# The GLA stage of a hybrid decoder step in another order: early output tiles between the near products

## What is computed

```
def rec_mixer(...):
    hm, c, n, m = mlstm_chunkwise(...)
    hm = rms_norm(hm, m_norm_g) * jax.nn.sigmoid(mo)
    log_a = jax.nn.log_sigmoid((glr @ w_gate_up + b_gate)) / G_GATE_TAU
    hg, s = gla_chunked(gq * G_KEY_DIM ** -0.5, gk, gv, log_a, s0)
    hg = rms_norm(hg, g_norm_g) * jax.nn.silu(gg)
    mix = jnp.concatenate([hm, hg], axis=-1)
    return mix @ w_out, c, n, m, s

def gla_chunked(q, k, v, log_a, s0):       # one chunk of it
    bc = jnp.cumsum(lac, axis=2)
    o_inter = einsum('bhtk,bhkv->bhtv', qc * exp(bc), s)
    decay = exp(where(mask, bc[:, :, :, None, :] - bc[:, :, None, :, :], -inf))
    a = einsum('bhtk,bhsk,bhtsk->bhts', qc, kc, decay)
    o = o_inter + einsum('bhts,bhsv->bhtv', a, vc)
    s_new = exp(b_end)[..., None] * s + einsum('bhsk,bhsv->bhkv', kc * exp(b_end - bc), vc)
```

## Time and profile before

| | us |
|---|---|
| median of 3 runs | 1524.04 |
| lowest, highest | 1517.58, 1527.65 |
| the profiled execution | 1523.02 |
| its span in the trace | 1521.4 |
| mean granted clock of TensorE | 0.957 of full |
| PE busy (matmul) | 1421.0 (93%) |
| DVE busy | 844.3 (55%) |
| ACT busy | 524.2 (34%) |
| POOL busy | 100.4 (7%) |

### The profile page before, as it was taken

How to read it: one execution, slowest core, us unless ns; L and a number is a source line. 1 busy time by engine, 2 the same in 40 slices (tenths; PEclk the granted TensorE clock), 3 DMA queues, 4 the chain that set the end, 5 groups by cost and what they waited for, 6 DMA issues and landing times.

```text
span 1521.4 us, 29729 instructions
## 1 busy us (share of the span) xinstructions
PE 1421.0 (93%) x11874; PEld 1349.3 (89%) x11874; DVE 844.3 (55%) x1277; ACT 524.2 (34%) x856; POOL 100.4 (7%) x138
## 2 busy tenths in 40 slices
PE   5999999788999999999999898997799999999997
PEld 4889899678999999999998677775699999999997
DVE  5355357564666666623253777778446666665221
ACT  4333434334333232322233454554243332322110
POOL 0021111112000000000000000000020000000000
PEclk9899999779999999999999999997799999999999
DMA  5443243212222223322126666773022222233320
GB/s 199 70 144 80 99 113 107 53 59 84 79 88 97 86 93 94 120 96 91 59 91 209 183 221 193 220 252 129 22 95 93 88 97 85 94 99 109 113 90 21
DMA packets 45820, 167.86 MB, mean 110 GB/s; under 512 B 5882, under 2 KB 7210, under 8 KB 45498
## 3 DMA queue, kind: packets, MB, share of 16 engines
q1 hardware_dynamic: 38506, 143.77, 29.0%
q0 software_dynamic: 7248, 23.15, 6.1%
HBM read 155.42 MB, written 11.48 MB: 110 GB/s over the span
## 4 chain that ended last, share of the span: by engine, by line
PE 84%; DVE 6%; issue 4%; ACT 4%; DMA 1%; POOL 0%; DVEq 0%; ACTq 0%; POOLq 0%
PE ps L516 55%; PE ps L567 13%; PE ps L696 2%; DVE mx L2084 1%; PE ps L925 1%; PE ps L1028 1%; ACT w_hi L1097 1%; ACT e_att L1455 1%; PE ps L631 1%; PE ps L879 1%; PE ps L1004 1%; PE ps L941 1%; PE ps L738 1%; PE ps L928 1%; DMA qb<-q_rows 1%
## 5 line engine op out<-in xcount | busy, mean ns | idle before, releaser
L516 PE MATMUL ps<-h_hi,w_hi 128*128 128x260 f32 x1616 | 459.4, 284 | 5.1 <-DVE h_lo L1562 4.6
L1553 DVE TENSOR_TENSOR w_lo<-raw,w_hi 128x1024 fp32r<-128x1024 f32 (+1 forms) x189 | 245.0, 1296 | 390.8 <-ACT w_hi L1097 390.8
L516 PE MATMUL ps<-h_hi,w_lo 128*128 128x260 f32 x1616 | 457.9, 283 | 0.0
L516 PE MATMUL ps<-h_lo,w_hi 128*128 128x260 f32 x1616 | 456.3, 282 | 0.0
L516 PEld LDWEIGHTS ps<-h_hi,w_hi 128*128 128x128 f32 x1616 | 305.4, 189 | 6.9 <-issue 4.4
L516 PEld LDWEIGHTS ps<-h_lo,w_hi 128*128 128x128 f32 x1616 | 305.2, 189 | 0.2
L516 PEld LDWEIGHTS ps<-h_hi,w_lo 128*128 128x128 f32 x1616 | 305.2, 189 | 0.0
L1097 ACT CAST w_hi<-raw 128x1024 fp32r<-128x1024 f32 (+1 forms) x189 | 208.0, 1101 | 224.3 <-PE ps L516 216.7
L516 PE MATMUL ps<-a_lo,w_hi 128*128 128x260 f32 x704 | 199.0, 283 | 0.0
L516 PE MATMUL ps<-a_hi,w_hi 128*128 128x260 f32 x704 | 198.8, 282 | 0.0
L516 PE MATMUL ps<-a_hi,w_lo 128*128 128x260 f32 x704 | 198.8, 282 | 0.0
(11 more groups left out here) (381 smaller groups left out, 2121.6 us busy)
## 6 DMA issues: line engine op xcount, KB each, us to landing
raw<-in_w_ffn SPq DMA_DIRECT2D x88, 512.0 KB, 3.4
raw<-in_w_down SPq DMA_DIRECT2D x32, 704.0 KB, 4.1
k_pages<-in_cache_k SPq DMA_DIRECT2D x32, 512.0 KB, 4.3
v_pages<-in_cache_v SPq DMA_DIRECT2D x32, 512.0 KB, 6.1
raw<-in_w_rec_in SPq DMA_DIRECT2D x29, 512.0 KB, 4.9
raw<-in_w_att_kv SPq DMA_DIRECT2D x24, 512.0 KB, 4.1
raw<-in_w_rec_out SPq DMA_DIRECT2D x8, 512.0 KB, 3.7
raw<-in_w_att_q SPq DMA_DIRECT2D x8, 512.0 KB, 3.5
```

Source lines behind the costliest of these rows:

```text
L516: ins = TE.matmul(half(bank, h), w_part[:, buf, w], m_part[:, k_at + k, h * HALF:(h + 1) * HALF], start=start, stop=stop)
L1553: V.tensor_tensor(w_lo[:, n % 2, 0:nk * P], raw[:, n % RAW, 0:nk * P], w_hi[:, n % 2, 0:nk * P].bitcast(F32), ALU.subtract).then_inc(lo_sp ...
```

## The change

It reorders and does not change what is computed.

- `early` becomes a generator that gives out one matmul at a time. `near_levels` takes such a generator and places one of its matmuls before every fourth near product. In pair 0 near A takes the last third (`h_lo` with `w_hi`) of early tiles 0 and 1, near B takes tile 2; in pair 1 near A takes tile 5, near B tile 6. What the generator has left after its 96 near products follows behind.
- Tiles 3, 4 and 7 are still done whole (`whole`), tile 3 behind `chunk_states(0)`, tile 4 behind `chunk_outputs(0)`, tile 7 ahead of `out_sums(1)`.
- `sample_outputs` moves from behind `chunk_outputs` to directly behind `within`.
- `exponents(0, "near")` moves ahead of the norm of the last mLSTM head on DVE, and `near_decays(0)` ahead of the conversion of the mLSTM rows on ACT.
- `sample_states` is split: its product (`sample_products`) moves ahead of `near`.
- In the late tiles the first halves of tiles 0 and 1 stand before the waits for the last GLA rows; the late tiles' PSUM banks are in another order (`LATE_BANK`).
- Splits of the slabs, and the drains, move to fit.

The core of the diff:

```diff
-            def early(m, bank, step=1):
+            def early(m, bank, step=1, terms=(0, 1, 2)):
...
+                            if t == 2 and k == KT // 2 - 1 and g == 1:
+                                ins.then_inc(slab_done if m % 2 else early_done, 1)
+                            yield
...
-            def near_levels(p, levels, at_bank):
+            def near_levels(p, levels, at_bank, beside, every):
...
                             for blk in range(4):
+                                if (4 * hh + blk) % every == every - 1:
+                                    next(beside, None)
...
-            early(0, 0)
+            whole(0, 0, terms=(0, 1))
...
-            early(1, 2, 5)
+            whole(1, 2, 5, (0, 1))
...
-                near_levels(p, (2, 3, 4), 3)
-                near_levels(p, (5, 6, 7), 5)
+                first, second = ((after_early(), early_behind(2, 2, 5, rD, "m1", 0)),
+                                 (early_behind(5, 0, 1, vA, "vt", 1), early_behind(6, 2, 5, oD, "tp1", 0)))[p]
+                near_levels(p, (2, 3, 4), 3, first, 4)
...
+                near_levels(p, (5, 6, 7), 5, second, 4)
...
-                if p:
-                    wait(pe, oD, "tp0", p - 1)
-                else:
-                    wait(pe, rD, "m1")
+                wait(pe, rD, "m6" if p else "m2")
...
             within(0)
+            sample_outputs(0)
+            chunk_states(0)
             wait(pe, gD, "n4", 0)
-            early(2, 3)
-            chunk_states(0)
-            wait(pe, rD, "m2")
-            early(3, 3)
-            chunk_outputs(0)
+            whole(3, 3)
             wait(pe, gA, "far", 0)
             v_chunks(1)
-            sample_outputs(0)
-            wait(pe, vA, "vt", 1)
-            early(4, 0)
+            chunk_outputs(0)
+            wait(pe, rD, "m3")
+            whole(4, 3)
             out_sums(0)
-            wait(pe, rD, "m4")
-            early(5, 0)
 
             within(1)
-            wait(pe, gD, "n4", 1)
-            early(6, 3)
+            sample_outputs(1)
             chunk_states(1)
             chunk_outputs(1)
-            sample_outputs(1)
+            wait(pe, gA, "far", 1)
+            whole(7, 0)
             out_sums(1)
-            wait(pe, gA, "far", 1)
-            early(7, 0)
             wait(pe, rD, "m7")
             wait(pe, oD, "lo1", 0)
             late(0, range(2))
-            wait(pe, oD, "lo0", 1)
-            late(0, range(2, 3))
-            wait(pe, oD, "lo1", 1)
-            late(0, range(3, 4))
             wait(pe, oA, "rms1", 1)
-            for c in range(1, S_OUT):
+            late(1, range(2))
+            for k in range(2):
+                wait(pe, oD, f"lo{k}", 1)
+                for c in range(2):
+                    late(c, range(2 + k, 3 + k))
+            for c in range(2, S_OUT):
                 late(c, range(KT // 2))
...
             size_of_decay(1)
             own_decay(0)
+            near_decays(0)
+            values(0)
             act.wait_ge(early_free, 1)
             wait(act, mD, "mix", M_HEADS - 1)
             S.copy(h_hi[:, 0:4, :], z[:, 12:16, :]).then_inc(hA.sem, 1)
-            values(0)
-            near_decays(0)
...
                     running(0)
+                    exponents(0, "near", 2, len(LEVELS))
                 rec_split(4)
```

More of the change, by code:

```diff
@@ L698, in early, with whole @@
                                             stop=t == 2 and k == KT // 2 - 1)
-                ins.then_inc(slab_done if m % 2 else early_done, 1)
+                            if t == 2 and k == KT // 2 - 1 and g == 1:
+                                ins.then_inc(slab_done if m % 2 else early_done, 1)
+                            yield
+            def whole(m, bank, step=1, terms=(0, 1, 2)):
+                for _ in early(m, bank, step, terms):
+                    pass
             def late(c, ks):
@@ L711, in late @@
                         for w_part, m_part in ((w_hi, h_hi), (w_hi, h_lo), (w_lo, h_hi)):
-                            ins = TE.matmul(half(2 * (c % 4), g), w_part[:, n % 2, w],
+                            ins = TE.matmul(half(LATE_BANK[c], g), w_part[:, n % 2, w],
                                             m_part[:, 4 + k, g * HALF:(g + 1) * HALF],
@@ L746, in _, with after_early, early_behind @@
             wait(pe, lA, "abs1")
-            early(1, 2, 5)
+            whole(1, 2, 5, (0, 1))
+            def after_early():
+                yield from early(0, 0, terms=(2,))
+                yield from early(1, 2, 5, (2,))
+            def early_behind(m, bank, step, steps, name, r):
+                wait(pe, steps, name, r)
+                yield from early(m, bank, step)
             def within(p):
@@ L756, in within @@
                     wait(pe, mA, "rms", M_HEADS - 1)
-                near_levels(p, (2, 3, 4), 3)
-                near_levels(p, (5, 6, 7), 5)
+                first, second = ((after_early(), early_behind(2, 2, 5, rD, "m1", 0)),
+                                 (early_behind(5, 0, 1, vA, "vt", 1), early_behind(6, 2, 5, oD, "tp1", 0)))[p]
+                near_levels(p, (2, 3, 4), 3, first, 4)
+                for _ in first:
+                    pass
+                near_levels(p, (5, 6, 7), 5, second, 4)
+                for _ in second:
+                    pass
                 wait(pe, dD, "qk_far", p)
@@ L786, in chunk_states @@
                 wait(pe, vA, "vt", p)
-                if p:
-                    wait(pe, oD, "tp1", p - 1)
                 for c in range(NC_G):
@@ L824, in out_sums @@
                 wait(pe, oA, "sq0", p)
-                wait(pe, rD, "m6" if p else "m3")
+                if p == 0:
+                    wait(pe, rD, "m4")
                 sums_of(3, 0)
@@ L1723, in cols_, with halves_of, exponents @@
                 return ap.unsqueeze(1).to_broadcast([P, n, ap.shape[1]])
+            def halves_of(ap, m):
+                v = ap.rearrange("p (n a m) -> p n a m", a=2, m=m)
+                return v[:, :, 0, :], v[:, :, 1, :]
+            def exponents(p, name, lo, hi):
+                wait(dve, dD, "bc", p)
+                if p:
+                    wait(dve, gP, "nearB" if name == "near" else "far", p - 1)
+                for l in range(lo, hi):
+                    m = LEVELS[l]
+                    early, late = halves_of(bc[:, :], m)
+                    to_early, to_late = halves_of(lev[:, l, :], m)
+                    edge = early[:, :, m - 1:m].to_broadcast([P, T // (2 * m), m])
+                    V.tensor_tensor(to_late, late, edge, ALU.subtract)
+                    ins = V.tensor_tensor(to_early, edge, early, ALU.subtract)
+                ins.then_inc(dD.sem, 1)
             def decay_input(p):
@@ L1831, in _ @@
                     rec_split(5)
-            def halves_of(ap, m):
-                v = ap.rearrange("p (n a m) -> p n a m", a=2, m=m)
-                return v[:, :, 0, :], v[:, :, 1, :]
-            def exponents(p, name, lo, hi):
-                wait(dve, dD, "bc", p)
-                if p:
-                    wait(dve, gP, "nearB" if name == "near" else "far", p - 1)
-                for l in range(lo, hi):
-                    m = LEVELS[l]
-                    early, late = halves_of(bc[:, :], m)
-                    to_early, to_late = halves_of(lev[:, l, :], m)
-                    edge = early[:, :, m - 1:m].to_broadcast([P, T // (2 * m), m])
-                    V.tensor_tensor(to_late, late, edge, ALU.subtract)
-                    ins = V.tensor_tensor(to_early, edge, early, ALU.subtract)
-                ins.then_inc(dD.sem, 1)
             def key_exponents(p):
@@ L1991, in _ @@
             end_factors(1)
-            early_drain(5, 0)
-            split("rec_out", 0, 3, KT)
+            sample_products(1)
             near(1)
-            early_drain(6, 3)
-            states(1)
+            early_drain(6, 2, 5)
             sample_states(1)
             split("rec_out", 0, 4, KT)
+            states(1)
             early_drain(7, 0)
@@ L2011, in late_drain @@
                 xc = x[:, c, :]
-                V.tensor_tensor(two(xc), two(xc), pair(2 * (c % 4)), ALU.add).then_inc(drained, 1)
+                V.tensor_tensor(two(xc), two(xc), pair(LATE_BANK[c]), ALU.add).then_inc(drained, 1)
                 if c < KT // 2 or c == KT - 1:
```

55 lines of the change are left out of this document (30 added, 25 removed).

## The result

| | before | changed |
|---|---|---|
| median of the runs, us | 1521.5 (4 runs, 1517.6 to 1527.7) | 1563.6 (4 runs, 1561.6 to 1567.5) |
| span of the profiled execution, us | 1521.4 | 1561.6 |
| PE busy, us | 1421.0 | 1468.9 |

The changed kernel takes 1.028 times the time of the kernel before (interval 1.024 to 1.032): 42 us slower. The forecast was 1514 us, a gain of 9 us.

What follows compares the result with a forecast made beforehand. PE, 93% busy, was held up by instruction supply, the clock and a few waits. Late tiles would end at 343.9 + 6.0 + 20.2 = 370.1 us against 379.3, so 1523.0 - 9 = 1514 us, range 1505 to 1524.

Steps and rivals of the forecast that it cites:

- Start: Ahead of pair 0's near products: exponents before the last mLSTM norm, early tile 0 delayed 0.3 us, near start at 268.4 us.
- The unit of the weave: Near stages: eight near records and one early matmul, taken at 0.28 us, with bounds of 0.20 and 0.55 us.
- the other bound: Near stages: 0.55 us a unit, from a far group of six records of two sizes in 0.65 us at low clock.
- three signs of being wrong: Woven stretches: units over 0.4 us, granted clock of 0.5, or the late block not late any more.
- late block: Pair 0's near products: instruction block whose burst at 282.29 us came 4.77 us late; DMAs would still delay it.
- Stops for instructions: Near products: PE waits for blocks of 256 instructions, about 3.7 us each; the woven matmuls would fill the gaps.
- Clock: Behind the near stages: mixed clock, with far products at 4.0 us, samples 5.0 us and chunk states 1.0 us.
- the clock holds: Rival: woven stretches keep the clock up until the samples are done, 8 us more gain, 1506 us; chance 0.20.
- From tile 3 to pair 1: End of tile 3 to pair 1's near products: 11.8 us against 16.3 before, with PE idle for almost 4 us.
- Last part: After pair 1's sums: 6.0 us to the low half, then 168 late matmuls in 20.2 us.
- Weaving hides little: Rival, near stages: slower block arrival or mutual waits, 0.40 us a unit; gain 2 to 4 us, 1520 us; chance 0.18.
- The slower rival: Clock falls in the hole ahead of pair 1's near products, 0.56 us a unit there; 1527 us; chance 0.10.

Runs made afterwards that it cites:

- blocks of eight: Changed kernel with eight early matmuls woven after every 32 near products in place of one after every four; 1526.2 us, ratio 1.003 to the kernel before.
- the form without such waits: Changed kernel with every woven early matmul cut to a near product's form (64 x 32 weights, f32, 32 columns); 1532.0 us, one run.

## Why the prediction was wrong

*Start.* The near products were to start 4.1 us behind the first matmul of tile 0. They did after 4.0 us (260.3 to 264.29). Right. That all of it lay 4.1 us earlier than forecast is scatter of unchanged mLSTM code, as said above, and not the change.

*The unit of the weave: the step that failed.* I took 0.28 us, "near the lower end, because that end comes from the near products themselves". It measured 0.51 at full clock. That is near the other bound, 0.55 from the far group, which was the right kind of row: it alternates two sizes, and the near products do not. That the number fits so well is luck, because the bound halved a group of the low clock. With blocks of eight the far groups ran at a granted clock of 1.00 and took 0.44 us, not 0.325:

```profile
286.82 0.33 PE L795 MATMUL ps<-lev 64*64 64x64 f32 x2
...
287.26 0.32 PE L795 MATMUL ps<-lev 64*64 64x64 f32 x2
```

By the same working that is 0.07 us a record and 0.71 us a unit. I added start intervals of two streams that were never mixed. The experiments break the 0.51 down: 0.20 of work (0.08 + 0.12) and 0.31 at the two changes, of which 0.19 is the early matmul's weight load that nothing covers. Format alone makes the unit 0.32 with a short matmul, size on top 0.41, the columns 0.51. Stages of 15.2 and 13.4 us became 29.1 and 36.5; 48 units at 0.78 us are 37.4. All three signs of being wrong that the prediction names came: units above 0.4 us, a granted clock of 0.5, and no late block.

*Stops for instructions.* Right in kind, and worthless: they went, because PE needed longer than the instructions did. (The prediction reads 2.43 us as the stop behind the burst of 143 records. In the trace that burst is followed by one of 1.37 us, and 2.43 us is the next stop; nothing hangs on it.)

*Clock.* I took a mixed clock and far products of 4.0, samples 5.0 and states 1.0 us; they had half clock: 5.0, 6.16 and 1.98. In pair 1 everything between near stage and the end of the sums took 25.7 us (365.7 to 391.4) for 19.8 forecast. The rows showed half clock in this stage before as well; a mean between the levels was too kind. Halving the far groups to 2.6 us for the case "the clock holds" was wrong too: eight at 0.44 us are 3.5 us.

The Trainium skill ("TensorE: Matmul & The Clock Gate", section "HAM oscillation — how this bites in real kernels") puts the fall to the low clock down to waits between batches. Here the clock stood at 0.50 from 270 us on in a stretch in which the records show no idle time on PE; whether the waits inside a unit count as such is not told apart by any run. In the form without such waits the clock was 0.50 in pair 1 all the same, with three stops of 1.4 to 1.7 us in the near stage. The Trainium skill's floor of 25 ns on the same page (section "Wait — 56ns, not 53.3ns?") would make a unit 0.32 us, an estimate from that page; the near records of the blocks are 10 ns apart (64 in 0.68 us), so that floor isn't what was missing from the 0.51 us unit.

*From tile 3 to pair 1.* Forecast 11.8 us, "the near products wait for the last root"; measured 17.1 us (312.1 to 329.21). They do wait for the root (1.55 us), but the sums ahead of it waited 5.00 us for tile 4's drain. The code shows tile 4 on bank 3 and the sums' wait for `m4`; I counted the wait as met without walking down DVE's list to the drain. The idle of almost 4 us that I put ahead of the near products stood ahead of the sums.

*Last part.* Forecast 6.0 us from the sums to the resumed late tiles, then 20.2; measured 5.4 (391.4 to 396.82) and 20.4 us. Right.

*Rivals.* "Weaving hides little" named the mechanism, a full-size matmul that waits for the small ones and they for it, and priced it at 0.40 us for 1520. The slower rival had its point of decision at 0.47 us a unit, which was right for the balance; but I let only the clock get there. At full clock a unit is over it already. The slower rival had 0.10, and slower by more than 15 us 0.04. Both deserved much more, since one of the two bounds that I had written down (0.55) lay beyond that point.

*The sum again with what was measured.* Units at 0.51 us in place of 0.28: pair 1 24.5 - 13.4 = 11.1, pair 0 20.4 - 15.2 = 5.2, so 1514 becomes 1530 us, slower even at full clock. Half clock in the near stages: (36.5 - 24.5) + (29.1 - 20.4) = 20.7. From tile 3 to pair 1, the drain and the sums at half clock: 17.1 - 11.8 = 5.3. Half clock in the rest: 5.9 in pair 1, and 18.7 - 15.3 = 3.4 in pair 0. Together 1566 us, against 1563.6 measured; the early start (4.1 us less) and the 2.5 us more behind the late tiles, neither of them forecast, make up most of the difference.

## To carry to other kernels

Mixing two kinds of matmul is not priced by adding their start intervals: find a row where the kinds alternate, and if the bounds straddle the point at which the sign turns, say so in the chances. If products of another form must fill a stream of small tiles, put them there in blocks: eight at a time cost nothing here where one at a time cost 36 us. For each wait that a change adds, walk down the list of the engine that fulfils it to that very instruction.

## What the runs showed of the hardware

- Between small f32 matmuls on 64 x 32 tiles (10 ns apart among themselves) and an fp32r or full-size one, loads and products no longer overlap: the next weights are loaded only when the last product is almost through. From the first of eight near records to a woven matmul of another format or size it took 0.19 to 0.20 us, whichever of the two differed, against 0.08 us for the eight records; back it took the woven one's load and columns, one behind the other (0.13 to 0.32 us). Without a difference a near record starts 0.01 us behind the woven one. A unit was 0.095 us (nothing differs), 0.25 (128 columns on its own tile), 0.32 (format), 0.41 (format and size), 0.43 (format and 260 columns), 0.51 (all), 0.56 (size, 64 f32 columns).
- Records call this time "busy": PE 35.00 of 35.00 us in pair 1's near stage, where a unit's own work is at most twice 0.20 of its 0.78 us. A group's count against its time shows what busy time does not.
- At half clock the unit takes 0.78 us, 1.5 times and not twice as long.
- Supply of instructions: with units of 0.095 us there were 13.1 us of stops ahead of near products in the two pairs, with units of 0.51 us none.
- What decides when the clock falls stays open. It fell during the near products of pair 0 in the kernel before and in the versions with and without weaving, and came back at different times: with samples behind the chunk outputs it was 0.62 from 287 to 296 us and 1.00 from 296 to 303, with samples ahead 0.50 and 0.70. In pair 1's near stage it was 0.50 to 0.56 in every version that weaves there by ones or twos, the one without waits at changes among them, and 0.77 to 1.00 in every other, the kernel before included. No run varied the clock alone, so how the 36 us of the weaving divide into waits and clock is not shown; 88 units at 0.51 us would be 45 us where 66 were measured, so an estimate from these is 21 us of clock.
